# TensorE's program for eight experts: a loop over them, or eight copies in a row

## The reference

```python
def swiglu(h, w1, w3, w2):
    return (jax.nn.silu(h @ w1) * (h @ w3)) @ w2

def moe(h, router_w, router_b, w1, w3, w2):
    ...
    logits = (t @ router_w).astype(jnp.float32) + router_b.astype(jnp.float32)
    top_v, top_i = lax.top_k(logits, TOP_K)
    wts = jax.nn.softmax(top_v, axis=-1)
    gates = jnp.sum(jax.nn.one_hot(top_i, N_EXPERTS, dtype=jnp.float32) * wts[..., None], axis=1).astype(t.dtype)
    out = gates[:, 0:1] * swiglu(t, w1[0], w3[0], w2[0])
    for e in range(1, N_EXPERTS):
        out = out + gates[:, e:e + 1] * swiglu(t, w1[e], w3[e], w2[e])
```

## Time and profile before

| | us |
|---|---|
| runs: 1538.30, 1540.28, 1535.77; median | 1538.3 |
| the profiled execution | 1539.1 |
| its span | 1537.3 |
| TensorE's matmuls, busy | 1450.8 |
| TensorE's weight loads (beside the matmuls) | 1008.6 |
| VectorE, busy | 386.8 |
| ScalarE, busy | 272.9 |

### The profile page before, as it was taken

The page is one execution under the profiler, slowest core; times in us unless marked ns, Lnnn a source line. Parts: engine busy times, 40 slices in busy tenths (PEclk is TensorE's granted clock), DMA queues, the critical chain, the costliest instruction groups (busy, mean ns, idle before and its releaser), DMA issues.

```text
span 1537.3 us, 44498 instructions
## 1 busy us (share of the span) xinstructions
PE 1450.8 (94%) x20573; PEld 1008.6 (66%) x20573; DVE 386.8 (25%) x682; ACT 272.9 (18%) x381; POOL 16.4 (1%) x30
## 2 busy tenths in 40 slices
PE   6899898999798999899899989989989998999996
PEld 3888797999667756565565656656556565666554
DVE  2658654455354210010010010011001001001003
ACT  2433442333413100100100100010010011000002
POOL 1000000000000000000000000000000000000000
PEclk9799999999999899999999999999999999999998
DMA  9657657554437499699889979969979987998990
GB/s 358 243 184 294 257 241 302 205 180 179 163 136 302 175 386 393 244 390 390 330 318 380 364 292 392 384 262 385 398 288 362 381 354 293 386 385 324 393 388 30
DMA packets 65153, 465.48 MB, mean 303 GB/s; under 512 B 7572, under 2 KB 7736, under 8 KB 9032
## 3 DMA queue, kind: packets, MB, share of 16 engines
q1 hardware_dynamic: 64184, 460.82, 77.1%
q0 software_dynamic: 784, 1.75, 0.5%
HBM read 460.96 MB, written 1.57 MB: 301 GB/s over the span
## 4 chain that ended last, share of the span: by engine, by line
PE 89%; DMA 3%; DVE 3%; ACT 3%; issue 2%; SPq 0%; POOL 0%; DVEq 0%; ACTq 0%
PE ps L427 85%; DMA raw<-dense_stream 3%; PE ps L835 2%; ACT hT L1018 2%; DVE w_lo L1146 1%; ACT w_hi L993 1%; DVE rstd L1221 1%; PE ps L507 1%; PE ps L877 0%; PE ps L465 0%; DVE xT L1379 0%; PE ps L589 0%; ACT rnd L1023 0%; SPq L913 0%; DVE xT L1452 0%
## 5 line engine op out<-in xcount | busy, mean ns | idle before, releaser
L427 PE MATMUL ps<-raw,arena 128*32 128x256 f32 x16128 | 894.4, 383 | 28.5 <-issue 27.8
L427 PEld LDWEIGHTS ps<-raw,arena 128*32 128x32 f32 x16128 | 520.4, 111 | 384.7 <-issue 51.6
L427 PE MATMUL ps<-rnd,w_hi 128*128 128x256 f32 x1632 | 303.6, 288 | 9.5 <-DVE rnd L1232 8.8
L427 PEld LDWEIGHTS ps<-rnd,w_hi 128*128 128x128 f32 x1632 | 257.6, 194 | 17.1 <-issue 12.6
L427 PE MATMUL ps<-rnd,w_lo 128*128 128x256 f32 x816 | 233.2, 286 | 0.0
L1463 DVE TENSOR_TENSOR arena<-ps,arena 64x768 f32<-64x768 f32 x56 | 53.7, 960 | 565.4 <-ACT arena L1090 565.4
L1090 ACT ACTIVATE arena<-ps 64x768 f32<-64x768 f32 x56 | 45.0, 803 | 646.8 <-PE ps L427 646.8
L427 PEld LDWEIGHTS ps<-rnd,w_lo 128*128 128x128 f32 x816 | 158.3, 194 | 0.0
L1146 DVE TENSOR_TENSOR w_lo<-raw,w_hi 128x2048 fp32r<-128x2048 f32 x53 | 121.4, 2292 | 119.6 <-ACT w_hi L993 119.5
L993 ACT ACTIVATE w_hi<-raw 128x2048 fp32r<-128x2048 f32 x53 | 101.2, 1911 | 170.8 <-PE ps L427 113.9
L1474 DVE TENSOR_TENSOR arena<-ps,arena 128x512 f32<-128x512 f32 x32 | 19.9, 684 | 165.1 <-PE ps L427 165.1
(11 more groups left out here) (125 smaller groups left out, 466.2 us busy)
## 6 DMA issues: line engine op xcount, KB each, us to landing
raw<-moe_stream SPq DMA_DIRECT2D x336, 1024.0 KB, 6.9
raw<-dense_stream SPq DMA_DIRECT2D x101, 1024.0 KB, 6.4
out<-tok SPq DMA_DIRECT2D x4, 256.0 KB, 2.0
arena<-dft_constants POOLq DMA_DIRECT2D x1, 640.0 KB, 9.8
tok<-in_x_prompt SPq DMA_DIRECT2D x1, 512.0 KB, 5.3
tok<-in_x_sample SPq DMA_DIRECT2D x1, 512.0 KB, 6.1
out<-arena POOLq DMA_DIRECT2D x2, 256.0 KB, 3.5
cst<-shape_constants SPq DMA_DIRECT2D x1, 371.5 KB, 4.3
```

The source lines that it names most:

```text
L427: return pe.matmul(out, lhsT, rhs, start=first, stop=last, **kw)
```

## The change

TensorE's loop is replaced by eight calls of `expert` while the program is built, so its program holds eight copies of the body instead of one in a loop and one behind it. The instructions of a copy are the same, with constants where the loop had values that depend on the pass. The programs of ScalarE, VectorE, SyncE and GpSimd are as before, with their loops, and so is the part behind the experts.

```diff
         gather(0)
-        with pe.Fori(0, EXPERTS - 1) as e:
-            expert(e)
-        expert(EXPERTS - 1, last_one=True)
+        for e in range(EXPERTS):
+            expert(e, last_one=e == EXPERTS - 1)
         spread(EXPERTS + 1, EXPERTS + 1)
```

## The result

The changed kernel takes 1498.6 us in the median of four runs (1492.0 to 1500.9), the kernel before 1538.1 beside it: a ratio of 0.974, 95% interval 0.970 to 0.977. That is 39.5 us less, where 40.9 were forecast; the forecast was 1497.4.

The account below looks back on a forecast made before the run. TensorE, busy 94% of the span, was taken as the bound, with pauses at loop returns and slow clock behind them removable. −27.85 − 13.05 = −40.9 us from the 1538.3 us median gave 1497.4 us; range 1494.9 less 2, up to 1506.

Parts of the forecast that it names:

- The six returns: TensorE's idle time at the loop's six jumps back to its top, expected to go: 27.85 us.
- The slow clock: The 528 records behind each return, slowed by a lower clock, would run like the eighth expert's: 13.05 us gained.
- That the idle time is code: At a return TensorE waits to have again code that lies 268 KB behind; 4.36 to 4.84 us each.
- Rival A: Something unnamed at an expert's end holds TensorE whatever its program, so the pause stays: 1538 us; chance 0.04.
- The rule on branches: Skill page's 51 ns per branch, 108 ns per compare-and-branch; would make all six returns cost 1 us, no measurable change.
- The body and the longer program: Constants for iteration values inside the experts, and eight copies of the code instead of two, would cost 0.
- rival C: Code comes too late inside the eight bodies, 6.8 us a stop; one in every expert gives 1552 us; chance 0.03.
- The forecast that the code traffic stays about as it was: Code already comes in once per execution, so the instruction queue would still carry about 171 transfers.
- ScalarE and VectorE: They keep their loops; their returns stay covered at the spread and its adds, so cost 0.
- The weight transfers: Without pauses, weights still land in time inside the experts, 6.9 us against 16.0 us of cover: cost 0.
- Rival B: Weight transfers set the experts' pace below 365 GB/s; at 355 the time is 1523 us; chance 0.04.
- The total: Whole kernel: 40.9 us less, giving 1497.4 us, 2.7% less.

Follow-up runs that it names:

- e8_exit: Kernel before, TensorE's loop kept, its jump announced from a register: back in the first six passes, go on in the seventh; 1497.9 us, ratio 0.975.
- e4_skip: Changed kernel with a forward jump ahead of each expert but the first, four over a whole expert copy, three over one wait; 1522.1 us.
- e2_four: Kernel before with only the first four experts in TensorE's loop and the last four written out; 1519.5 us, ratio 0.988.
- e1_hint: Kernel before, TensorE's loop kept, with its jump back announced at the top of every pass, the last included; 1506.6 us, ratio 0.979.
- e3_near: Changed kernel with a one-wait TensorE loop ahead of each expert but the first, returning once at four places, 23 times at three; 1530.7 us.
- e6_all: Changed kernel with the loops of ScalarE and VectorE written out too; 1498.1 us, ratio 0.974.
- e7_slots: Changed kernel with three slots for the raw weights instead of seven; 1642.2 us.
- e5_sizes: Changed kernel with seven loops of three passes, bodies of 16 to 2048 transposes, added behind the last expert's spread; 3126.7 us.

## Why the prediction was right

*The six returns, 27.85 us.* Right: all of it went, and nothing came in its place.

*The slow clock, 13.05 us.* Right, and to be taken from the eighth expert, not the first: all seven stretches behind a passage took 28.84 us. 27.85 + 13.05 = 40.90 against 40.91 in the profiles.

*That the idle time is code.* This was argued from the size of the instruction transfers only; `e8_exit` shows it (the loop kept, the pause gone), and `e4_skip` from the other side (no loop, the pause there). The trace of the kernel before held a direct sight of it, which the prediction missed: the DMA queues in the window of its first pause alone, 634.28 to 639.00.

```profile
q8 instruction: 1, 0.02, 1.2%
```

All six pauses have such a transfer of 16 KB, at the same place: it begins 1.7 to 2.2 us after the last matmul and has ended 1.7 to 1.8 us before the next one. The pauses of `e2_four` and `e4_skip` and the one of `e1_hint` have one too (1.6 to 2.1 us after, 1.4 to 1.8 before); the 7.5 us of `e3_near`, made of near returns, have none. One transfer in a window would prove little, as they come some 7 us apart all through the experts; the same place in every far jump's pause is what counts. So a pause is the wait for one 16 KB transfer, some 2.0 us until it begins, 0.9 for itself and 1.7 until TensorE goes on, and not for the 268 KB of a body; the rest comes while TensorE works. Rival A is refuted with it, and by `e2_four`. The rule on branches in the Trainium skill ("Advanced Engine Details and Errata", Control Flow Timing), weighed in the prediction, prices the jump alone. The short jumps of `e4_skip` and the single returns of `e3_near` show no pause, so the 4.4 to 4.8 us are not the jump's.

*The body and the longer program, 0.* Right: 31.22 us for twelve pieces in every copy, no stop inside a copy, so rival C did not come. The forecast that the code traffic stays about as it was came out a little off: 163 transfers for 171. The 8 that went are 1.3 for each return.

*ScalarE and VectorE, 0.* Right, by the chain and by `e6_all`. VectorE's idle time ahead of the spread's adds fell by 165.1 − 124.1 = 41.0 us, as it only waits for TensorE.

*The weight transfers, 0.* Right: 362 GB/s over the experts, landings of 7.1 us against 16.0 of cover. Rival B did not come; `e7_slots` shows the size of that cover and what comes without it.

*The total* is off by 1.2 us, less than the runs of one kernel lie apart.

## What to carry to other kernels

A pause that ends on "issue" and returns with the period of a loop is a sign of code that has to be fetched again, if the DMA queues show an instruction transfer in its window (the pauses of `e3_near` end on "issue" too and have none); a place in the same trace where the program goes straight on tells beforehand what is left without it. A long loop body can be written out, or its jump can be announced, but then the exit has to be announced rightly too. A pause on TensorE is to be priced with the slow stretch behind it: those of 3.9 to 7.6 us had one of 1.5 to 3.1 us, in the loop half as much again, while behind those of 1.4 to 1.9 us in `e5_sizes` the granted clock stayed at 1.00.

## What had not been expected

An announcement that is wrong once costs nearly what it saves at one return: 3.94 us of pause and 2.03 of slow clock where straight code had none. Bodies of up to 1024 instructions returned without any pause, and a far return with no weights on the move cost 1.4 to 1.9 us instead of 4.4 to 4.8. And most of what makes the runs of one kernel differ lies ahead of the experts: eleven profiles put their beginning anywhere from 509.8 to 519.4 us, while a passage without a pause took 36.75 us wherever one was recorded.
